# Memory keys and two gate groups of a two-layer decoder trunk: token-major chunks in place of feature-major halves

## The reference, cut to what matters

```python
(r_q, r_k, r_v, a_cq, a_ckv, a_kpe, l_x, l_v, l_o, l_i, l_f, c_q, z) = _split_cols(x @ w_in, IN_SPLITS)
k, v = jnp.split(mem @ w_mem_kv, 2, axis=-1)              # memory attention: keys and values
y = jnp.concatenate([ret, mla, mls, memo], axis=-1) * jax.nn.silu(z.astype(f32))
y = y.astype(x.dtype) @ w_out
return _layernorm(DEEPNORM_ALPHA * x + y, ln_g, ln_b)
```

## Time and profile before

| | us |
|---|---|
| median of three runs | 902.78 |
| the runs | 901.48, 902.78, 1107.38 |
| the profiled execution, its own time | 902.31 |
| its span in the profile | 900.5 |
| TensorE busy | 893.0 |
| VectorE busy | 659.0 |
| ScalarE busy | 490.5 |

### The profile page before, as it was taken

One profiled execution on the slowest core, in us unless ns is written; L12 is line 12 of the kernel. 1 busy time (PEld: TensorE's weight loads), 2 busy tenths in 40 slices (PEclk: granted clock), 3 DMA queues, 4 the chain that ended last, 5 costly groups with the idle time before them and its releaser, 6 DMA issues.

```text
span 900.5 us, 13869 instructions
## 1 busy us (share of the span) xinstructions
PE 893.0 (99%) x4836; PEld 776.0 (86%) x4836; DVE 659.0 (73%) x1308; ACT 490.5 (54%) x926; POOL 16.0 (2%) x18
## 2 busy tenths in 40 slices
PE   9999999999999999999999999999999999999997
PEld 7888998888888888888888889888888888888896
DVE  6878776877775776666659787778779567787865
ACT  6665864545545455544476657746355544555541
POOL 0000000000000000000000000000000000000001
PEclk9999999999999999999999999999999999999999
DMA  9785556546787676665554865574485964766922
GB/s 358 280 318 162 148 160 234 187 141 216 240 231 253 214 211 213 194 194 198 189 188 143 307 223 159 171 252 163 154 256 166 282 180 163 234 199 230 339 98 94
DMA packets 62452, 187.75 MB, mean 208 GB/s; under 512 B 7336, under 2 KB 15792, under 8 KB 61744
## 3 DMA queue, kind: packets, MB, share of 16 engines
q1 hardware_dynamic: 61808, 185.82, 62.9%
q10 hardware_dynamic: 576, 1.05, 0.3%
HBM read 177.13 MB, written 9.71 MB: 207 GB/s over the span
## 4 chain that ended last, share of the span: by engine, by line
PE 95%; DMA 2%; issue 1%; ACT 1%; DVE 0%; SPq 0%; POOL 0%; POOLq 0%; ACTq 0%; DVEq 0%
PE acc L1319 22%; PE acc L1304 17%; PE acc L1305 17%; PE acc L1308 17%; PE acc L1325 11%; PE work L1061 1%; PE work L1060 1%; PE work L1059 1%; PE work L1054 1%; DMA B<-turn 1%; DMA B<-mrow 1%; PE work L1209 1%; PE work L1208 1%; DMA B<-in_mem_t 0%; PE work L1220 0%
## 5 line engine op out<-in xcount | busy, mean ns | idle before, releaser
L1391 DVE TENSOR_TENSOR lo<-raw,hi 128x512 fp32r<-128x512 f32 (+2 forms) x607 | 386.4, 657 | 185.2 <-ACT hi L1018 174.7
L1018 ACT ACTIVATE hi<-raw 128x512 fp32r<-128x512 f32 (+2 forms) x607 | 351.8, 603 | 279.0 <-PE acc L1308 160.0
L1304 PE MATMUL acc<-hi,xx 128*128 128x512 f32 (+2 forms) x576 | 212.5, 373 | 0.4 <-ACT hi L1018 0.4
L1305 PE MATMUL acc<-hi,xx 128*128 128x512 f32 (+2 forms) x576 | 209.0, 366 | 0.0
L1319 PE MATMUL acc<-xx,hi 128*128 128x512 f32 x768 | 193.3, 393 | 0.4 <-ACT hi L1018 0.4
L1308 PE MATMUL acc<-lo,xx 128*128 128x512 f32 (+2 forms) x576 | 163.9, 366 | 0.0
L1319 PEld LDWEIGHTS acc<-xx,hi 128*128 128x128 f32 x768 | 138.1, 189 | 25.4 <-issue 0.5
L1304 PEld LDWEIGHTS acc<-hi,xx 128*128 128x128 f32 x576 | 108.5, 188 | 17.2 <-issue 0.8
L1305 PEld LDWEIGHTS acc<-hi,xx 128*128 128x128 f32 x576 | 108.6, 189 | 16.3
L1308 PEld LDWEIGHTS acc<-lo,xx 128*128 128x128 f32 x576 | 104.3, 188 | 17.4
L1325 PEld LDWEIGHTS acc<-xx,lo 128*128 128x128 f32 x768 | 104.8, 190 | 7.5
(11 more groups left out here) (349 smaller groups left out, 1030.2 us busy)
## 6 DMA issues: line engine op xcount, KB each, us to landing
raw<-in_w SPq DMA_DIRECT2D x263, 512.0 KB, 3.8
raw<-in_w SPq DMA_DIRECT2D x26, 256.0 KB, 2.7
raw<-in_w SPq DMA_DIRECT2D x16, 328.0 KB, 3.1
B<-turn SPq DMA_DIRECT2D x40, 128.0 KB, 3.9
turn<-B SPq DMA_DIRECT2D x6, 512.0 KB, 5.8
Y<-in_wuq SPq DMA_DIRECT2D x2, 1152.0 KB, 8.5
Y<-in_x_t SPq DMA_DIRECT2D x4, 512.0 KB, 8.7
turn<-Y SPq DMA_DIRECT2D x4, 512.0 KB, 6.5
```

Of the source, the lines that this page charges most:

```text
L1018: act.activation(place(l, t, hi), raw[:, s, (t % 2) * w:(t % 2 + 1) * w], ACT.Copy)\
L1304: pe.matmul(o, ah[:, q], hi[:, s, 0:w], start=k == 0, stop=False, skip_group_check=name == "memv")
L1305: pe.matmul(o, al[:, q], hi[:, s, 0:w], start=False, stop=False, skip_group_check=name == "memv")
L1391: dve.tensor_tensor(place(l, t, lo), raw[:, s, (t % 2) * w:(t % 2 + 1) * w], place(l, t, hi).bitcast(F32), ALU.subtract).then_inc(lo_done. ...
```

## The change

- `memk0`, `memk1` become one token chunk `memk` of 16 slots, and so do z3 and z2. The weights are stored in the other order for them. z1, z0, lx and cq stay as feature halves.
- The steps `part` and `joined` of these six halves go. In their place VectorE transposes the squares straight from PSUM (`turn` at its slots 36, 196 and 213), waits for itself and gives the PSUM place free. SP writes them at pairs 23, 102 and 111 and reads them back at 26, 105 and 114; retention's read moves from pair 114 to 116.
- The keys' high and low parts are made from the turned tile, at slots 51 to 53 instead of 30 to 39. SiLU of z3 and z2 reads the turned tile and moves from 190, 198, 206, 214 to 208, 209, 226, 227, and the gatings and the y parts behind it move too.
- The four loads of x in layer 0 move from pairs 99 to 105 to pairs 117 to 123.
- SP waits for the gating of z3 before it reads z2 back, since both use one place.

```diff
-CHUNKS = [("memv", W, "tok"), *_halves("memk", "lx", "cq"),
+CHUNKS = [("memv", W, "tok"), ("memk", W, "tok"), *_halves("lx", "cq"),
...
-          ("rq", W, "tok"), ("rk", W, "tok"), ("rv", W, "tok"), *_halves("z3_", "z2_", "z1_", "z0_"),
+          ("rq", W, "tok"), ("rk", W, "tok"), ("rv", W, "tok"), 
+          ("z3", W, "tok"), ("z2", W, "tok"), *_halves("z1_", "z0_"),
...
-        (28, "part", "memk", 0), (36, "part", "memk", 1), (44, "part", "lx", 0), (52, "part", "lx", 1),
+        (44, "part", "lx", 0), (52, "part", "lx", 1),
...
-        (188, "part", "z3_", 0), (196, "part", "z3_", 1), (204, "part", "z2_", 0), (212, "part", "z2_", 1),
...
-        (30, "memk", 0), (38, "memk", 1),
+        (51, "memk", 0), (52, "memk", 1),
...
-        (190, "silu", 3, 0), (198, "silu", 3, 1), (206, "silu", 2, 0), (214, "silu", 2, 1),
-        (222, "silu", 1, 0), (230, "silu", 1, 1), (238, "silu", 0, 0), (246, "silu", 0, 1),
-        (205, "y_hi", 0), (207, "y_hi", 1), (221, "y_hi", 2), (223, "y_hi", 3),
+        (208, "silu", 3, 0), (209, "silu", 3, 1), (226, "silu", 2, 0), (227, "silu", 2, 1),
+        (229, "silu", 1, 0), (232, "silu", 1, 1), (238, "silu", 0, 0), (246, "silu", 0, 1),
+        (213, "y_hi", 0), (214, "y_hi", 1), (232, "y_hi", 2), (234, "y_hi", 3),
...
-        (29, "joined", "memk", 0), (37, "joined", "memk", 1), (45, "joined", "lx", 0), (53, "joined", "lx", 1),
+        (36, "turn", "memk"), (196, "turn", "z3"), (213, "turn", "z2"), (45, "joined", "lx", 0), (53, "joined", "lx", 1),
...
-        (31, "lo", "memk", 0), (39, "lo", "memk", 1), (63, "lo", "cq", 0), (71, "lo", "cq", 1),
+        (52, "lo", "memk", 0), (53, "lo", "memk", 1), (63, "lo", "cq", 0), (71, "lo", "cq", 1),
...
-        (202, "ret_stats", 0), (204, "ret_norm", 0), (212, "ret_stats", 1), (214, "ret_norm", 1), (215, "turn", "ret"),
-        (192, "gate", 3, 0), (200, "gate", 3, 1), (208, "gate", 2, 0), (216, "gate", 2, 1),
-        (224, "gate", 1, 0), (232, "gate", 1, 1), (240, "gate", 0, 0), (248, "gate", 0, 1),
-        (206, "y_lo", 0), (208, "y_lo", 1), (222, "y_lo", 2), (224, "y_lo", 3),
+        (202, "ret_stats", 0), (204, "ret_norm", 0), (212, "ret_stats", 1), (214, "ret_norm", 1), (216, "turn", "ret"),
+        (210, "gate", 3, 0), (211, "gate", 3, 1), (228, "gate", 2, 0), (230, "gate", 2, 1),
+        (232, "gate", 1, 0), (234, "gate", 1, 1), (240, "gate", 0, 0), (248, "gate", 0, 1),
+        (214, "y_lo", 0), (215, "y_lo", 1), (233, "y_lo", 2), (235, "y_lo", 3),
...
-TURN_OUT_AT = {74: "rot", 57: "c", 77: "cell", 81: "rq", 89: "mla0", 90: "rk", 95: "mla1", 112: "ret"}
-TURN_IN_AT = {76: "rot", 59: "c", 79: "cell", 83: "rq", 92: "mla0", 93: "rk", 98: "mla1", 114: "ret"}
+READ_FROM_ACC = ("memk", "z3", "z2")
+TURN_OUT_AT = {23: "memk", 57: "c", 74: "rot", 77: "cell", 81: "rq", 89: "mla0", 90: "rk", 95: "mla1",
+               102: "z3", 111: "z2", 112: "ret"}
+TURN_IN_AT = {26: "memk", 59: "c", 76: "rot", 79: "cell", 83: "rq", 92: "mla0", 93: "rk", 98: "mla1",
+              105: "z3", 114: "z2", 116: "ret"}
...
+        for g in (3, 2):
+            squares[f"z{g}"], turn_to[f"z{g}"] = Y[:, g * 1024:(g + 1) * 1024], B[5][:, 0:1024]
+        squares["memk"], turn_to["memk"] = B[8][:, 0:1024], B[7][:, 0:1024]
...
-                    if l == 0 and m in (99, 101, 103, 105):
+                    if l == 0 and m in (117, 119, 121, 123):
                         wait_job(sp, l, ("mla_qn", 1))
-                        load_x(sp, (m - 99) // 2)
+                        load_x(sp, (m - 117) // 2)
...
+                        if name == "z2":
+                            sp.wait_ge(gated.sem, gated.at(l, 1))
...
                 def silu(g, i):
+                    if g >= 2:
+                        wait_turned(act, l, f"z{g}")
+                        act.activation(by_square(yT[:, 4 * g:4 * g + 4, :], i), turned_tokens(f"z{g}", i), ACT.Silu)\
+                           .then_inc(silu_done.sem, 1)
+                        return
...
+                    if name in READ_FROM_ACC:
+                        wait_chunk(dve, l, CI[name])
+                    if name in ("z3", "z2"):
+                        last = {"z3": "rk", "z2": "mla1"}[name]
+                        dve.wait_ge(turn_out[last].sem, turn_out[last].at(l, 0))
+                    src = acc[:, acc_turn(l, CI[name])[1], :, :].rearrange("p i n -> p (i n)") if name in READ_FROM_ACC \
+                        else turn_from[name]
                     dve.transpose(squares[name].rearrange("p (b k r) -> p k b r", b=4, r=32),
...
+                    if name in READ_FROM_ACC:
+                        dve.wait_ge(squared[name].sem, squared[name].at(l, 0))
+                        dve.sem_inc(acc_sem(l, name), 2)
```

More of the change, by code:

```diff
@@ L228 @@
         (193, "ret_weigh", 0), (195, "ret_weigh", 1), (203, "ret_weigh", 2), (205, "ret_weigh", 3),
-        (202, "ret_stats", 0), (204, "ret_norm", 0), (212, "ret_stats", 1), (214, "ret_norm", 1), (215, "turn", "ret"),
-        (192, "gate", 3, 0), (200, "gate", 3, 1), (208, "gate", 2, 0), (216, "gate", 2, 1),
-        (224, "gate", 1, 0), (232, "gate", 1, 1), (240, "gate", 0, 0), (248, "gate", 0, 1),
-        (206, "y_lo", 0), (208, "y_lo", 1), (222, "y_lo", 2), (224, "y_lo", 3),
+        (202, "ret_stats", 0), (204, "ret_norm", 0), (212, "ret_stats", 1), (214, "ret_norm", 1), (216, "turn", "ret"),
+        (210, "gate", 3, 0), (211, "gate", 3, 1), (228, "gate", 2, 0), (230, "gate", 2, 1),
+        (232, "gate", 1, 0), (234, "gate", 1, 1), (240, "gate", 0, 0), (248, "gate", 0, 1),
+        (214, "y_lo", 0), (215, "y_lo", 1), (233, "y_lo", 2), (235, "y_lo", 3),
         (244, "y_lo", 4), (245, "y_lo", 5), (251, "y_lo", 6), (252, "y_lo", 7)]:
     _put(DVE_AT, _s, *_step)
-TURNS = ("c", "cell", "rq", "rk", "ret", "rot", "mla0", "mla1")
+TURNS = ("c", "cell", "rq", "rk", "ret", "rot", "mla0", "mla1", "memk", "z3", "z2")
 TURN_COLS = {n: 6 * P if n == "rot" or n[:3] == "mla" else 4 * SEQ for n in TURNS}
-TURN_OUT_AT = {74: "rot", 57: "c", 77: "cell", 81: "rq", 89: "mla0", 90: "rk", 95: "mla1", 112: "ret"}
-TURN_IN_AT = {76: "rot", 59: "c", 79: "cell", 83: "rq", 92: "mla0", 93: "rk", 98: "mla1", 114: "ret"}
+READ_FROM_ACC = ("memk", "z3", "z2")
[3 more added lines that the diff above has]
+              105: "z3", 114: "z2", 116: "ret"}
 KEPT_PAIRS = (4, 5, 6, 7, 0, 1, 2, 3)
@@ L427, in build_trunk, with turned_tokens, by_square @@
         squares["mla1"], turn_to["mla1"] = Y[:, 2048:2048 + 6 * P], B[7][:, 0:6 * P]
+        for g in (3, 2):
+            squares[f"z{g}"], turn_to[f"z{g}"] = Y[:, g * 1024:(g + 1) * 1024], B[5][:, 0:1024]
+        squares["memk"], turn_to["memk"] = B[8][:, 0:1024], B[7][:, 0:1024]
+        def turned_tokens(name, i):
+            return turn_to[name].rearrange("p (a i j r) -> p i j a r", a=4, i=NT, j=4)[:, i]
+        def by_square(buf, i):
+            return buf[:, :, i * P:(i + 1) * P].rearrange("p j (a r) -> p j a r", a=4)
         def turned_head(name, h):
@@ L459, in build_trunk @@
         acc_read = [signal(f"acc_read{p}", 0, before=2) for p in range(2)]
-        joined, lo_part = signal("joined", 14), signal("lo_part", 14)
+        joined, lo_part = signal("joined", 8), signal("lo_part", 8)
         kq_split = signal("kq_split", 4)
@@ L505, in build_trunk @@
         roped = signal("roped", 4)
-        squared = {n: signal(f"squared_{n}", 2 if n[:3] in ("mem", "mla") else 1) for n in TURNS}
+        squared = {n: signal(f"squared_{n}", 2 if n in ("mla0", "mla1") else 1) for n in TURNS}
         turn_out = {n: signal(f"turn_out_{n}", 1, step=16) for n in TURNS}
@@ L586, in A @@
             return acc[:, acc_turn(l, CI[name])[1], i, :]
-        JOINED = [("memk", 0), ("memk", 1), ("lx", 0), ("lx", 1), ("cq", 0), ("cq", 1),
-                  *((f"z{g}_", q) for g in (3, 2, 1, 0) for q in range(2))]
+        JOINED = [("lx", 0), ("lx", 1), ("cq", 0), ("cq", 1), ("z1_", 0), ("z1_", 1), ("z0_", 0), ("z0_", 1)]
         def wait_joined(eng, l, name, q):
@@ L599, in sums @@
                 return yT[:, 4 * int(name[1]) + 2 * q:4 * int(name[1]) + 2 * q + 2, :]
-            return heads({"memk": B[8], "cq": B[5]}[name])[:, 2 * q:2 * q + 2, :]
+            return heads(B[5])[:, 2 * q:2 * q + 2, :]
         def uq_high(l):
@@ L624, in operand @@
                 h, rest = {"memk": mKT, "cq": cQT}[name]
+                if name == "memk":
+                    return turned_tokens(name, i), by_square(h, i), by_square(rest, i), kq_split.sem
                 return sums(name, i), h[:, 2 * i:2 * i + 2, :], rest[:, 2 * i:2 * i + 2, :], kq_split.sem
@@ L694, in _ @@
                     if l == 1 and m == 32:
-                        wait_chunk(sp, l, CI["memk1"])
+                        wait_chunk(sp, l, CI["memk"])
                         sp.dma_start(gb0_place[:, :], a["gb"][0:1, :].partition_broadcast(P).rearrange("p o n -> p (o n)"))\
@@ L862, in go @@
                             act.wait_ge(c_scaled.sem, c_scaled.at(l, 1))
```

(18 more changed lines are left out.)

## The result

The changed kernel took 904.59 us (median of 9 runs, 901.05 to 907.10), the kernel before 901.81 us in the runs beside it (9 runs). The ratio is 1.0024, 95% interval 1.0014 to 1.0034: some 2.2 us slower (2.8 by the medians; the ratio is not that of the medians), where 2.9 us faster was forecast. By the 2% bound it counts as no change, but the time lies above the stated range of 897.6 to 903.0 and on the other side. The profiled execution took 907.1 us, with a span of 905.3.

The account below looks back on a forecast made before the run. TensorE, busy 893.0 of 900.5 us, was taken as the bound, so time is its instructions' sum. Form -3.50, jobs +0.64 and +0.5, stall -0.54 make -2.9: 902.3 to 899.4 us, range 897.6 to 903.0.

Parts of the forecast that it names:

- The form of the chunks: 96 slots of memory keys, z3 and z2 go from 1.3965 to 1.360 us each: 3.50 us less.
- The rival that only columns count: Form worth nothing, since only the 3072 columns of either form set a slot's time: 902.9 us; chance 0.04.
- Jobs between the slots: TensorE's other jobs cost more between token slots: +0.64 us for eight transpose jobs in layer 1, about +0.5 in z3 and z2.
- The stall at slot 184: Layer 1: TensorE's wait for `hi` behind the late turned retention keys goes, as token form wants one tile first: -0.54 us.
- The transpose out of PSUM: VectorE's square transpose of 128x1024 from PSUM: 1.24 us taken, bounds 1.24 to 1.37, plus 0.2 for its wait.
- The keys' path, "Price: nothing": Slots 36 to 61: turned keys land at 516.2, say up to 518, before ScalarE needs them; no cost.
- My limit for the last read, 518.8: Layer 1: latest landing of the turned keys that keeps TensorE's slot 52 (521.70) on time; slack 1 to 2.6 us.
- The reserve that I read off `lo` 61: VectorE after the keys' low parts: `lo` 61, wanted at 535.2, keeps 1.5 of its 2.6 us.
- The rival "turned keys come late": Last read lands past 518.8, each microsecond beyond costing TensorE one, in both layers: 906.0 us; chance 0.12.
- z2, "Slack 2.7 us": Slots 213 to 227: z2's reads land at 21.2 us after slot 208's start, limit 23.9 for slot 226; price nothing.
- The sum: Whole kernel: -3.50 + 0.64 + 0.5 - 0.54 = -2.9 us, giving 899.4 us; chance 0.58.
- part eaten: Rival: z2, the keys or VectorE's reserve past its limit by 1.5 to 3 us over both layers: 901 to 902.4; chance 0.17.

Follow-up runs that it names:

- both mends: The changed kernel with the keys' splits moved behind the convolution (slots 55, 57, 64, 66) and retention's exchange and x loads later; 899.06 us, ratio 0.9963 against before.

## Why the prediction was wrong

**The form of the chunks: right.** By the earlier trace rows a changed chunk gives 16 x 0.0365 = 0.58 us; layer 0's keys gave 0.56 without a wait. For z3 and z2, slot 208 started 2.35 us ahead of before in layer 0 (314.29 before, 311.94 with both mends). Of this 0.13 is the start, 0.56 the keys and 0.66 a stall of before that I had not priced (below); 1.0 is left, forecast 2 x 0.58 - 0.25 = 0.92. The rival that only columns count is out: it gave 902.9 where the mended kernel took 899.06. So is the size that the 2.5 ns of the Trainium skill, "TensorE: Matmul & The Clock Gate", section "Back-to-back issue gap", would give: an estimated 0.5 us for all 96 slots. The same section of the Trainium skill says that this formula, which is for a single matmul, counts too little where short matmuls each load weights; the trace agrees with some 18 ns for each further one, and I had passed that over.

**Jobs between the slots: right, a little dear.** A transpose job and two token slots repeat every 3.20 us in the mended kernel (466.90, 470.11, 473.31), so the job costs 3.20 - 2.72 = 0.48, not 0.52. The eight jobs cost +0.4 over what they cost before (0.58 - 0.15), not +0.64.

**The stall at slot 184: right.** No wait of TensorE between 700 and 760 in the changed kernel.

**The transpose out of PSUM: right.** 1.24 us at 500.58 and 1.25 us at 320.94, the lower end of the bounds.

**The keys' path, "Price: nothing": this step failed, in its limit first and in its landing second.** My limit for the last read, 518.8, came from slot 52 (521.70). For slot 52 it held: on that clock ScalarE's copy of the keys ran at 519.3 in layer 0 of the changed kernel, where slot 52 waited 0.23 us, and at 517.7 in layer 1, where it did not wait. But the copy holds a longer path as well. Behind it come `hi` 52 and 53 and with them the start of VectorE's convolution; behind that `joined` of cq's first half at slot 61; ScalarE's copy of it stands ahead of `hi` 63; and the feature pair at slot 62 wants `hi` 63 before its first matmul. That is 5.4 + 14.0 = 19.4 us from the copy to slot 62, which is due 5 x 2.793 = 13.96 us after slot 52. So the limit was 516.2, and my own landing, 516.2 to 518, already gave up to 1.8 us a layer. The reserve that I read off `lo` 61 as 1.5 us was 0.2: in the kernel before it is 14.22 us from the MEMSET (77.98) to the pair, and 14.02 where the pair waits.

The landing was late too. The squares' write took 10.72 and 9.45 us where I had 9.0, and the last read 6.36 and 6.04 where I had 3.9. Together slot 62 came 94.51 - (74.73 + 2.79 + 13.96) = 3.03 us late in layer 0 and 541.58 - (526.17 + 13.96) = 1.45 in layer 1, which is what the copy at 519.3 and 517.7 was past 516.2 to a tenth. The low parts, which I had at 1.1 us, make 0.54 of each.

The rival "turned keys come late" had the right transfer and the wrong place: ten slots later the price is paid. That its 906.0 us is near the measured 904.59 is in part luck, for of the 7.0 us above 1.62 are the clock's and 1.76 z2's, which it did not count.

**z2, "Slack 2.7 us": failed in a size.** The limit held; the landing was mis-sized. Counted from slot 208 (317.08 in the changed kernel) the last read was issued at 18.3, where I had 17.3, and its data were there at 25.8, where I had 21.2 by a median of 3.9 us. The chain of the changed kernel has that read, nearly as long as the 8.21 us of the earlier trace rows:

```profile
334.94 7.96 DMA B<-turn
```

Retention's write had been issued 3.5 us ahead of the reads, at 329.14. With both mends it follows them: the reads are issued at the same distance from slot 208 (327.51 - 311.94 = 15.6 us), and the longest takes 6.2 us. In the four profiled kernels with the write ahead (the change and three experiments) slot 226 waits in seven of eight layers, from 0.19 to 1.76 us; in the three with it behind, in none of six. Retention's read back was moved with the write, so which of the two it is stays open; the loads of x are not it, for the first was issued at 345.21 in the changed kernel, when z2's data were there, and layer 1 has none.

**The sum.** Forecast -2.9, measured -2.7 by the medians once both causes are away (3.3 faster by the ratio, 2.3 to 4.4 by its interval). In the change itself 7.0 us of waits and lowered clock stand against it in the profiled execution; by the medians 904.59 - 899.06 = 5.5 us. I had let "part eaten" and "keys late" have 0.29 together, as if apart: they share ScalarE and VectorE, so both came.

**A wait of before that I left out.** I named one `hi` wait of 0.4 us between the start and the tail; there were two, by the kernel before's timeline:

```profile
154.42 0.47 PE L1304 MATMUL acc<-hi,xx 128*128 128x512 f32 x1 [0.40 <-ACT hi L1018]
```

It cost 0.66 us with the late matmuls about it. In the profiled executions of the other kernels the wait of token slots for `hi` in the stretch after slot 64 was between nothing and 1.2 us; in this one ScalarE stood for VectorE, and VectorE for the mask's rows from DRAM (`B<-mrow`), which it got at 152.45. No edit here was aimed at it, so it is in the spread of single profiles, and the medians are the ones to go by: spans say 900.5 - 896.5 = 4.0 us between the kernel before and the mended one, the medians 2.7.

**Open.** Why the clock fell after the stall of 1.99 us in the changed kernel, but not after 1.90 us at the same pair in another. And why the keys' exchange takes up to 2.1 us more in one execution than in another with the same instructions before it; that would fit the spread of the changed kernel's runs, 901 to 907 us, but no run here shows it.

## What to carry to other kernels

When work that waits for a transfer is moved into an in-order engine's queue, its limit isn't that of the nearest tile: list every instruction that the engine passes to another one in the next ten slots, follow each through the second engine's order to TensorE, and take the earliest limit. Here the nearest gave 518.8 and the path over VectorE's convolution 516.2, and 2.6 us were the difference between no price and a loss. A DRAM exchange under load is to be planned by its worst landing beside another write, not by the median. Moving the keys' four splits, retention's exchange and the loads of x turned a loss of 2 us into a gain of 3.

## What the runs showed of the hardware

- Over the same 3072 columns, six matmuls of 512 take 1.360 us and four of 512 with four of 256 take 1.3965, also where a chunk is changed from the one to the other: some 18 ns for each further matmul with its weight load.
- A 32x32 square transpose of 128x1024 fp32 takes VectorE 1.24 us, from PSUM (1.24 and 1.25) as from SBUF.
- After a wait of 1.99 us the granted clock fell to 0.91 and then 0.66 in windows of 4 us and cost 1.62 us; after waits of 1.90, 1.77, 1.76 and 1.27 us it stayed at 1.00.
- A DRAM exchange of 512 KB under the weights' stream: the keys' write landed after 10.72 and 9.45 us and a last read of 128 KB after 6.36 and 6.04, against medians of 5.8 and 3.9 us in the kernel before. z2's last read took 7.96 us with another 512 KB write issued 3.5 us ahead of the reads and 6.2 with it behind them.
